# Sample attention of a hybrid decoder step: pages and tables made ready earlier, the bias added on VectorE, sequences joined one by one

## What is computed

```python
def dsa_sample(q, kv, qi, ki, wi, cache_kv, cache_idx_k, page_table):
    ...
    scores = _index_scores(qi, ki_all, wi)
    ...
    _, sel = lax.top_k(jnp.where(causal[None], scores, -jnp.inf), n_sel)
    ...
    phys = page_table[bidx, sel_past // PAGE_SIZE]
    kv_past = cache_kv[phys, sel_past % PAGE_SIZE]
    ...
    return _sparse_attend(q, kv_sel, valid)

def _sparse_attend(q, kv_sel, valid):
    ...
    s = jnp.einsum('bqkgd,bqnkd->bqkgn', qg, ks) * (A_HEAD_DIM ** -0.5)
    s = jnp.where(valid[:, :, None, None, :], s, -jnp.inf)
    p = jax.nn.softmax(s, axis=-1)
    o = jnp.einsum('bqkgn,bqnkd->bqkgd', p, vs)
    return o.reshape(B, Q, A_WIDTH).astype(q.dtype)
```

## Time and profile before

| what | value |
|---|---|
| median of 3 runs | 3584.91 us (3572.67 to 3586.05) |
| the profiled execution's own time | 3590.75 us |
| its span | 3588.7 us, 73930 instructions |
| mean granted TensorE clock | 0.92 |
| TensorE busy | 3311.3 us (92%) |
| VectorE busy | 2148.4 us (60%) |
| ScalarE busy | 1096.0 us (31%) |
| POOL busy | 488.6 us (14%) |
| DMA | 229.76 MB, mean 64 GB/s |

### The profile page before, as it was taken

One profiled execution on the slowest core, in us unless ns is written; L12 is line 12 of the kernel. 1 busy time (PEld: TensorE's weight loads), 2 busy tenths in 40 slices (PEclk: granted clock), 3 DMA queues, 4 the chain that ended last, 5 costly groups with the idle time before them and its releaser, 6 DMA issues. The chain is left out here.

```text
span 3588.7 us, 73930 instructions
## 1 busy us (share of the span) xinstructions
PE 3311.3 (92%) x29593; PEld 1990.2 (55%) x29593; DVE 2148.4 (60%) x4302; ACT 1096.0 (31%) x2337; POOL 488.6 (14%) x687
## 2 busy tenths in 40 slices
PE   8999999999999999699998657888886899999998
PEld 4544445555555555366665436667765555555553
DVE  2028889999999999487765435565653344432211
ACT  4136650000000000255553126555552111111211
POOL 3330000000000000000000413343432100000000
PEclk9999999999999999799999877776665999999999
DMA  5241111111111111211000931221211511121110
GB/s 156 74 104 49 42 48 55 55 55 59 58 55 55 55 61 44 68 45 28 22 19 13 290 111 41 52 55 49 54 29 41 186 62 62 62 74 62 47 39 24
DMA packets 217448, 229.76 MB, mean 64 GB/s; under 512 B 28473, under 2 KB 195316, under 8 KB 216612
## 3 DMA queue, kind: packets, MB, share of 16 engines
q1 hardware_dynamic: 149624, 110.52, 11.4%
q0 software_dynamic: 21328, 52.96, 5.1%
q10 hardware_dynamic: 46172, 61.71, 5.0%
HBM read 156.58 MB, written 68.52 MB: 63 GB/s over the span
## 5 line engine op out<-in xcount | busy, mean ns | idle before, releaser
L409 PE MATMUL fro_acc<-h_t,fro_w 128*128 128x416 f32 x3280 | 1176.2, 516 | 0.0
L409 PEld LDWEIGHTS fro_acc<-h_t,fro_w 128*128 128x128 f32 x3280 | 615.3, 190 | 543.5 <-issue 536.6
L692 DVE TENSOR_SCALAR_CACHE_REDUCE fro_work<-scores,fro_real 128x384 uint8<-128x384 f32 (+6 forms) x462 | 656.2, 1474 | 2.1
L516 ACT ACTIVATE fro_out<-fro_acc 128x416 f32<-128x416 f32 (+3 forms) x230 | 118.0, 513 | 793.9 <-PE fro_acc L409 711.4
L2134 PE MATMUL mrg_po<-mrg_wo,mrg_mrg 128*128 128x512 f32 (+1 forms) x544 | 238.2, 596 | 4.5 <-DVE mrg_mrg L2239 4.5
L2970 DVE CUSTOM_DVE_ANT_0 att_seen<-att_ps,scores 128x512 f32<-128x512 f32 (+3 forms) x320 | 181.3, 607 | 97.1 <-PE att_ps L2856 96.9
L2166 PE MATMUL mrg_pg<-mrg_wg,mrg_x_t 128*128 128x512 f32 (+1 forms) x544 | 236.3, 592 | 0.0
L658 DVE SCALAR_TENSOR_TENSOR scores<-fro_work,w_idx,scores 128x512 f32<-128x512 f32 (+3 forms) x280 | 187.9, 671 | 40.1 <-ACT fro_work L573 13.2
L2134 PEld LDWEIGHTS mrg_po<-mrg_wo,mrg_mrg 128*128 128x128 f32 (+1 forms) x544 | 101.1, 186 | 138.7 <-issue 133.8
L2940 ACT ACTIVATE att_seen<-att_seen,att_shift 128x128 f32<-128x128 f32 (+15 forms) x128 | 152.6, 1194 | 81.0 <-DVE att_shift L2978 81.0
L573 ACT ACTIVATE fro_work<-fro_wk 128x512 f32<-128x512 f32 (+3 forms) x320 | 144.5, 540 | 92.5 <-PE fro_wk L482 91.6
(11 more groups left out here) (440 smaller groups left out, 4669.8 us busy)
## 6 DMA issues: line engine op xcount, KB each, us to landing
z_t<-fro_out ACTq DMA_DIRECT2D x180, 208.0 KB
fro_w<-in_w_in SPq DMA_DIRECT2D x41, 512.0 KB, 4.2
mrg_m_in<-z_t POOLq DMA_DIRECT2D x56, 256.0 KB, 3.4
sat_kv<-in_cache_kv SPq DMA_DIRECT2D x96, 128.0 KB, 3.4
sat_kv<-in_cache_kv POOLq DMA_DIRECT2D x96, 128.0 KB, 3.6
rwk_zi<-z_t SPq DMA_DIRECT2D x80, 129.0 KB, 2.7
z_t<-fro_out ACTq DMA_DIRECT2D x45, 192.0 KB
scores<-in_x_prompt SPq DMA_DIRECT2D x16, 512.0 KB, 8.3
```

Of the source, the lines that this page charges most:

```text
L409: last = pe.matmul(acc[e % 2][:, 0:CW], w[block_no % 3][:, kk, :], h_t[:, kk, CW * g:CW * g + CW], start=(kk == 0), stop=(kk == KD - 1))
L692: chain.mark(dve.tensor_scalar(junk[b % 2][:, 0:n], scores[:, c:c + n], realf[:, b:b + 1], None, op, ALU.add, accum_out=count[:, b:b + 1]))
```

## The change

- `SampleReady` holds what the sample's attention finds ready: `qd`, `qf`, `same`, `own`, the page table, and `bw`, the bias of every sequence by head in bfloat16, 128 partitions x 8 x 4 x 257, with its copy in DRAM.
- In the start stage SP loads the page table. VectorE makes the bias (now bfloat16) ahead of the shifted rows. POOL stores it to DRAM eight times, once for each head, 263 KB each, ahead of its token rows. VectorE makes `own` at the end.
- In the prompt's attention SP loads `bw` with four DMAs of 526 KB ahead of its first gates. POOL makes `qd`, `qf` and `same` behind its selection table. Behind each block's two stores POOL loads pages into the columns of `scores` that have been read: 60 pages in all, those of sequence 0 and 28 of sequence 1.
- In the sample's attention `scores` serves as the first two page buffers. The bias products are gone; the maximum is an operation that adds `bw`, writes the sum to `seen` and takes the maximum. Each sequence's peaks, weights, join, division and turning are done beside the next sequence. TensorE weighs sequence b-1 between quarter 1 and quarter 2 of the scores of b. VectorE's list puts the peak behind quarter 0, the difference behind quarter 1, and the keep, which now needs ScalarE's exponential of the weight, ahead of the maximum. ScalarE takes that exponential behind its page loads.

The core of the diff:

```diff
+class SampleReady:
+    PAGES = 60
...
+        self.bw = sb("sat_bw", [P, SB, 4, 257], BF16)
+        self.bias = nc.dram_tensor("sat_bias", [4, SB, ST, AH, 4 * 257], BF16).ap()
...
@@ stage_sample_start, sync @@
+            sp.dma_start(early.table[:, :], t["page_table"].rearrange("b n -> (b n)").rearrange("(o n) -> o n", o=1)).then_inc(tab_in, 16)
             sp.wait_ge(ready, 1)
...
@@ stage_sample_start, gpsimd @@
+            pool.wait_ge(masked, 2)
+            for h in range(AH):
+                pool.dma_start(by_row[:, h, :], bias[:, :, :].rearrange("p k o -> p (k o)")).then_inc(mask_out, 16)
             pool.wait_ge(copied_a, 3)
...
+            pool.wait_ge(mask_out, 16 * AH)
...
@@ stage_sample_start, vector @@
+            chain.catch_up()
+            dve.tensor_copy(bias[:, :, 0:256].rearrange("p k (x i) -> p k x i", i=32),
+                            whole[:, 0:QK].rearrange("p (x k i) -> p k x i", k=4, i=32)).then_inc(masked, 1)
+            dve.tensor_copy(bias[:, :, 256:257].rearrange("p k o -> p (k o)"), whole[:, QK:QK + ST]).then_inc(masked, 1)
             dve.wait_ge(shifted, 1)
...
@@ stage_attend, sync @@
+            for g in range(4):
+                sp.dma_start(early.bw[32 * g:32 * g + 32, :, :, :].rearrange("p b k o -> p b (k o)"),
+                             early.bias[g].rearrange("b t h c -> (t h) b c")).then_inc(bias_in, 16)
             for b in range(NT):
...
@@ stage_attend, gpsimd @@
+            sample_tables(pool)
...
+                for a in range(pages_at(b), pages_at(b + 1)):
+                    page = pool.value_load(early.table[0:1, a:a + 1], min_val=0, max_val=t["cache_kv"].shape[1] - 1)
+                    pool.dma_start(scores[:, 2 * P * a:2 * P * a + 2 * P], kv_rows[bass.ds(page, 1), :, :].rearrange("o p c -> p (o c)"))\
+                        .then_inc(page_in, 16)
...
@@ stage_sample_attend, tensor @@
+            pe.wait_ge(cleared, 1)
+            for b in range(SB + 1):
+                if b < SB:
+                    scores_of(b, 0)
+                if b >= 2:
+                    turn_out(b - 2)
                 if b:
+                    turn_peaks(b - 1)
+                if b < SB:
+                    scores_of(b, 1)
                 if b:
+                    spread_peaks(b - 1)
                     weigh(b - 1)
+                if b < SB:
+                    scores_of(b, 2)
+                    scores_of(b, 3)
+                    new_scores(b)
+                if b:
+                    join(b - 1)
+            turn_out(SB - 1)
...
@@ stage_sample_attend, scalar @@
-                if b + 2 < SB:
+                if BUFS <= b + 2 < SB:
                     load_pages(act, b + 2, 2)
+                act.wait_ge(w_sub, b + 1)
+                act.activation(wgt[:, b:b + 1], wgt[:, b:b + 1], ACT.Exp, scale=scale).then_inc(w_ok, 1)
...
@@ stage_sample_attend, vector @@
             def keep(b):
                 dve.wait_ge(weighed, b + 1)
+                dve.wait_ge(w_ok, b + 1)
...
+            def mask(b):
+                dve.wait_ge(scored, b + 1)
...
+                dve.tensor_tensor_reduce(seen[b % 2][:, :, :], ps[:, :, 0:257], bw[:, b, :, :], 1.0, -3.4e38, ALU.add, ALU.max,
+                                         accum_out=most[:, b:b + 1]).then_inc(s_read, 1)
...
+            for b in range(SB + 1):
+                if b < SB:
+                    turn_keys(b, 0)
+                if b:
+                    peak_of(b - 1)
+                if b < SB:
+                    turn_keys(b, 1)
+                if b:
+                    below_peak(b - 1)
+                if b < SB:
+                    turn_keys(b, 2)
+                    turn_keys(b, 3)
...
                 if b:
                     keep(b - 1)
+                if b < SB:
+                    mask(b)
+                if b:
+                    finish(b - 1)
```

More of the change, by code:

```diff
@@ L2369, in __init__, with stage_sample_start @@
         self.bias, self.gate = const("rws_bias", [P, 4, NS]), const("rws_gate", [P, 4, NS])
-def stage_sample_start(nc, t, k, z_t, z_s, part, bias, ahead, rest):
+def stage_sample_start(nc, t, k, z_t, z_s, part, ahead, rest, early):
     QK = PAST // 4
@@ L2519, in stage_sample_attend @@
     SHARE = (slice(0, 3), slice(3, 6), slice(6, 8))
+    scale = float(HD ** -0.5)
     with Stage(nc, "sat") as s:
-        table = s.sb("table", [1, SB * NPG], I32)
-        kv = [s.sb(f"kv{i}", [P, NPG, 2 * P]) for i in range(BUFS)]
+        table, qd, qf, same, own, bw = early.table, early.qd, early.qf, early.same, early.own, early.bw
+        held = scores[:, 0:2 * NPG * 2 * P].rearrange("p (i a c) -> p i a c", i=2, c=2 * P)
+        kv = [held[:, 0, :, :], held[:, 1, :, :], s.sb("kv2", [P, NPG, 2 * P])[:, :, :]]
@@ L2529, in stage_sample_attend @@
-        parts, same = s.sb("parts", [P, SB, P]), s.sb("same", [P, NS])
-        peak, peaks, wgt = s.sb("peak", [SB, NS]), s.sb("peaks", [SB, 4, NS]), s.sb("wgt", [P, SB])
-        row, rowf, own = s.sb("row", [NS, 1], I32), s.sb("rowf", [NS, 1]), s.sb("own", [NS, 2])
-        inv, o, o_2 = s.sb("inv", [NS, SB]), s.sb("o", [NS, SB, P]), s.sb("o_2", [NS, SB, 2, HD])
+        most, less, sum_a, sum_b, wgt = (s.sb(n, [P, SB]) for n in ("most", "less", "sum_a", "sum_b", "wgt"))
+        parts = [s.sb(f"parts{i}", [P, P + 1]) for i in range(2)]
@@ L2595, in weigh, with turn_peaks @@
                   .then_inc(weighed, 1)
[L2597 to L2607 removed]
+            def turn_peaks(b):
+                pe.wait_ge(s_read, b + 1)
+                pe.transpose(end[0:1, 0:P], most[:, b:b + 1], k.ident[:, :]).then_inc(m_turned, 1)
@@ L2617, in _ @@
-                for n in range(ST):
-                    last = pe.matmul(ps[rows(3), n, 256:257], qf[:, b, :, :, :].rearrange("p t v g -> p (t v g)"), z_s[:, Z_K, b, 1 + n:2 + n],
-                                     start=False, stop=True, skip_group_check=True)
-                last.then_inc(scored, 1)
-            weigh(SB - 1)
-            pe.wait_ge(peaked, SB)
-            pe.transpose(end[0:SB, 0:P], most[:, :], k.ident[:, :]).then_inc(m_turned, 1)
-            pe.wait_ge(peak_ok, 2)
-            pe.matmul(end[:, 256:256 + SB], peaks[:, :, :].rearrange("b g q -> b (g q)"), k.ident[0:SB, 0:SB], start=True, stop=True)\
-              .then_inc(spread, 1)
@@ new lines, in turn_keys @@
+            def turn_keys(b, g):
+                for who in range(3):
+                    if b > 1:
+                        dve.wait_ge(kv_in[b % BUFS][g][who], 16 * (SHARE[who].stop - SHARE[who].start) * (b // BUFS + (b % BUFS == 2)))
+                if b == 1 and g == 3:
+                    dve.wait_ge(rest_in, 16 * (NPG - FIRST))
+                if b and g == 0:
+                    dve.wait_ge(scored, b)
+                dve.transpose(kt[:, GP * g:GP * g + GP, :], kv[b % BUFS][:, GP * g:GP * g + GP, 0:P]).then_inc(turned, 1)
```

272 lines of the change are left out of this document (139 added, 133 removed).

## The result

The changed kernel takes **3625.88 us** (median of 4 runs, 3620.69 to 3627.58), the kernel before 3581.35 us beside it (4 runs, 3572.67 to 3586.05). The ratio is 1.0127, with a 95% interval of 1.0104 to 1.0151: slower by 1.3%. The forecast of 3596 lay 0.3% above the 3584.91 it started from, and 3625.88 lies above its range of 3570 to 3618.

What follows compares the result with a forecast made beforehand. TensorE's chain, not the loads, was taken to close the sample's attention loop. Terms -17.5 + 29.7 - 8 + 6 + 1 = +11.2 took the profiled 3590.75 to 3601.9; with the median 5.8 lower, forecast 3596, range 3570 to 3618.

Steps and rivals of the forecast that it cites:

- the loop's term: Sample's attention, first to last maximum: lockstep, held keep and partly lowered clock make it 142.1 us against 112.4, +29.7.
- The gates' term: Start of the prompt's attention: gates land later behind 2.1 MB of bias loads, ScalarE's tanh waits, +6 us (0 to 9).
- D: Rival at the prompt's attention's start: bias loads cost 9 to 15 us, or no delay; 3590 to 3605; chance 0.08.
- the start: Sample's attention up to its first maximum: tables and 60 pages already ready, -17.5 us (-14 to -20).
- the start stage: Sample's start stage: two copies moved ahead of the shifted rows and POOL's added stores, +1 us (0 to 4).
- the end: Sample's attention after its last maximum: joins run per sequence, leaving 12.2 us, -8 us (-6.5 to -9.6).
- the remaining loads: Sample's attention: 196 page loads of 128 KB take 85 us, under the loop's 142, and were costed at nothing.
- B: Rival in the loop: the clock stays lowered and TensorE sets every period; total +39, 3624 us; chance 0.19.
- C: Rival in the loop: ScalarE's load issues don't hold; periods 15.5 us, total -22.4, 3562 us; chance 0.12.
- A: Rival in the loop: full clock, periods 18.6 and 15.5 us, loop +11.7, total -6.8, 3578 us; chance 0.16.
- the keep's releaser: Sign in the loop: the keep is released by ScalarE's weight exponential right after its eight load issues.
- the 9 us: Sign at the start of the sample's attention: the first maximum comes 9 us into the stage.

Runs made afterwards that it cites:

- the gates' experiment: Changed kernel with only the four bias-table loads moved in SP's list behind the gates of block 1 of the prompt's attention; one run 3604.69 us beside 3592.93.

## Why the prediction was wrong

**The failed step is the loop's term**, +29.7 in the forecast, +45.5 measured; within its bounds of 12 to 58, but the value taken was too low. It failed where the period with loads was taken at 21.3, with a lowered clock for only "most of the first half": it measured 23.9. Of these 2.6 us, 1.5 lie between 21.3 and the forecast's own lowered sum of 22.8, and 1.1 above that sum. Its mechanisms were the right ones: the lockstep, the keep held by ScalarE's issues, and the lowered first half are all in the rows. The sizes were not.

1. "A quarter of scores takes 1.2 at the full clock (4.8/4)". It takes 1.93 alone; dividing a run of four by four was the error. In a run, two take 2.84 and four 4.86, so each further quarter adds 0.9 to 1.0 us, and about 1 us (an estimate from these three) is paid once a run, however long it is. At the lowered clock it takes 3.3 to 3.64, not the 2.6 that was taken below a row showing 2.89. Two quarters a period stand alone in the chain. At the full clock, maximum to copied probabilities is 11.7 us (2005.57 to 2017.27), forecast 10.5; the 1.5 of the two quarters more than explain it. With the lowered first half it is 15.2 (2003.14 to 2018.35), forecast 14.7: here the dearer quarters were partly paid back, since the clock was up again for the turning of the probabilities.
2. The block of loads was priced from its own start: 7.4. It measured 7.15 to 7.85 (as forecast), but began 0.6 to 0.9 us after the copies.
3. "So I take the lowered clock for most of the first half: 21.3" split a difference between 18.6 and 22.8, though the earlier trace rows read 0.50 and 0.56 after shorter waits than the new loop has. Every period with loads had a lowered first half. 2.6 us a period, five times, is 13; the other two periods give the remaining 2.8 (38.4 against 35.6).

In this trace the granted clock is 0.50 to 0.53 in the first half of the periods with loads, and 1.00 behind. By the Trainium skill, TensorE: Matmul & The Clock Gate, section HAM oscillation — how this bites in real kernels, a long wait in every pass makes every pass begin at the lower clock; the trace agrees, with 0.50 from 2010 to 2015 and from 2030 to 2040. The 153.4 that the forecast worked out by it is 4.5 short of the 157.9 measured, its own 142.1 is 15.8 short. So the Trainium skill's rule was the better guide.

**The gates' term** was +6, measured +11.3. The forecast let the gates land at 1501 to 1503 of before, 10 to 12 us into the stage; they were there 14.0 us in (the tanh at 1501.61, with the stage beginning at 1487.64), where the tanh stood 4.8 us in before (1495.52 from 1490.75). That is 9.2 us, the upper bound already; 1.9 of it pass before SP issues the gates' loads at all. The stage lost 2.1 more behind it, where TensorE's clock was still lowered; that the 2.1 are this clock isn't shown. What D named, 9 to 15 us there, took place, with a chance of 0.08 in the forecast.

**Right were** the start (-17.5, measured -17.9), the start stage (+1, +0.5), the end (-8, -6.8: 13.5 us between the full sum of 10.6 and the lowered one of 13.7, near the second, with the last weighing lowered), the maximum with the addition in it (1.3, measured 1.22), POOL's tables and page loads at nothing (for the tables, as far as the gates' experiment shows it), and the remaining loads hidden.

**The sum of the misses**: loop +15.8, gates +5.3, end +1.2, start -0.4, start stage -0.5, unchanged stages +4.7; the profiled execution lies 1.7 us over its median, while 5.8 were subtracted: +4.1; and 0.5 us less of it lies outside the span: -0.5. Together 29.7, against 3625.88 - 3596 = 29.9; the rest is rounding. Without the 4.7 of the unchanged stages and these 4.1, which no term foresaw, the forecast would still be some 21 us short, but 3617 would have lain just inside the range: how far out the result fell is in part chance.

**The rivals.** B, at 3624, hit the time, not the cause. It put the decision in TensorE's path once the weighing is lowered too; in the rows the weighing takes 1.95 and the keep is released by ScalarE. C fell twice: the issues hold (7.85 us, keep 8.06 idle), and with the hold taken away the periods are 19.6, not 15.5. A's state, the full clock, was made by unused products, and its price was too low as well: with the hold its periods are 20.2 to 20.8 and one of 23.6, for 18.6; without it 16.87, for 15.5, in which the two quarters are 1.5. Of the signs named ahead, the keep's releaser, the clock of 0.50, the 9 us, and ScalarE idle at the first tanh came as said; of 18 us without loads one of two did (18.06, 20.37); the 21 us with loads (23.9) and the 12 us of the end (13.5) did not.

What no run settles is why the unedited stages differ by several microseconds between profiles, and what makes the prompt's attention 476.4 to 480.5 when the gates are first, and 484.8 to 489.3 when they aren't.

## What to carry to other kernels

Before work is moved from a long hidden run into the gaps between small dependent pieces, walk through one whole period of the new order with every hand-over between engines: here 3.65 us of products a sequence were removed and the loop still grew by 45 us, because two quarters, two turnings and a peak came to stand in one chain, in which the held exponential and the lowered clock then counted in full. Weighing first, with the four quarters together, made it 14 us shorter than before (98.0 against 112.4). A lone group of products is priced from a row in which it stands alone, not from a run of them divided by their number. A small operation that others wait for goes ahead of its engine's DMA issues, and on a queue what is needed in 10 us goes ahead of what is needed in 500.

## What the runs showed of the hardware

- The sixteen products of 32 x 32 x 256 that make one quarter's scores take 1.93 us alone, 2.84 for two quarters in a row (2020.29 to 2023.13), and 4.86 for four (2025.07 to 2029.93 in the reordered loop), all at the full clock. At the lowered one a lone quarter took 3.3 to 3.64.
- Products that nothing reads kept the granted clock at 1.00 over a loop that otherwise reads 0.73, and the loop was shorter with them: by 17.9 us with 30 a period, by 19.9 with 18 a period where the exponential stood first (0.81 without them). Ahead of an instruction that another engine waits for, they took part of it back (130.6 against 117.0).
- A load of 128 KB whose page number ScalarE reads itself took 0.9 to 1.0 us of its stream in the changed kernel (8 in 7.15 to 7.85), with the DMA engines busy for 0.58 of the time from 2019 to 2027, in the longest block, and 0.63 from 2043.2 to 2050.2. Over all runs blocks of eight took 7.1 to 8.9.
- Loads of 128 KB, issued on SP behind four of 514 KB, took 11.2 us to land, 3.1 with nothing ahead; issued first they cost ScalarE no wait.
